# State space phase: a group's squares and state stores issued in the next group, its variances and normalization one chunk later

## The reference

```python
def step(h, inp):                       # one chunk
    decay = exp(where(causal, acum_l - acum_s, -inf))
    y = einsum((cc @ bc) * decay, xc) + einsum(cc, h) * exp(acum)
    h = exp(acum[-1]) * h + einsum(bc, to_end * xc)
    return h, y
y = y + d_skip * xs
y = y * silu(z)
y = y * rsqrt(mean(y * y over a group's 256 channels) + EPS)
y = y * norm_g                          # outputs: y, and the final h of prompt and samples
```

## Time and profile before

| | |
|---|---|
| median of three runs | 5301.94 us (5300.33 to 5302.54) |
| the profiled execution | 5307.53 us |
| its span, first to last instruction | 5305.7 us |
| busy share of the span | PE 87%, DVE 68%, ACT 34%, POOL 29% |
| mean granted TensorE clock | 0.93 |

### The profile page before, as it was taken

One profiled execution on the slowest core, in us unless ns is written; L12 is line 12 of the kernel. 1 busy time (PEld: TensorE's weight loads), 2 busy tenths in 40 slices (PEclk: granted clock), 3 DMA queues, 4 the chain that ended last, 5 costly groups with the idle time before them and its releaser, 6 DMA issues. The chain is left out here.

```text
span 5305.7 us, 83850 instructions
## 1 busy us (share of the span) xinstructions
PE 4605.5 (87%) x28787; PEld 4251.3 (80%) x28787; DVE 3586.0 (68%) x6877; ACT 1782.4 (34%) x3697; POOL 1526.5 (29%) x1356
## 2 busy tenths in 40 slices
PE   5999999788887969874888376999999999999995
PEld 3999999677775649873887366999999999999994
DVE  3011555454554641234599997999999999999997
ACT  3111333323232641111444394333333333333332
POOL 0000000111110000000000002777777777777773
PEclk8999999888887889997999798999999999999997
DMA  3332222222222232342999157999999999999995
GB/s 134 126 135 84 83 89 89 113 105 104 105 105 73 53 114 92 134 150 83 357 351 334 68 197 248 358 366 364 368 361 362 371 362 362 367 363 365 369 361 197
DMA packets 349645, 1170.31 MB, mean 221 GB/s; under 512 B 40000, under 2 KB 91328, under 8 KB 342080
## 3 DMA queue, kind: packets, MB, share of 16 engines
q0 software_dynamic: 147456, 536.94, 27.2%
q1 hardware_dynamic: 159328, 483.07, 25.6%
q10 hardware_dynamic: 42720, 148.52, 7.3%
HBM read 971.20 MB, written 197.46 MB: 220 GB/s over the span
## 5 line engine op out<-in xcount | busy, mean ns | idle before, releaser
L2027 POOL DMA_INDIRECT ex_vr<-in_expert_v,ex_at x512 | 655.2, 1280 | 229.8 <-issue 152.8
L2025 POOL DMA_INDIRECT ex_ur<-scr_u_rows,ex_at x512 | 594.2, 1161 | 312.0 <-DVE ex_ur L2202 131.5
L2210 DVE SCALAR_TENSOR_TENSOR ex_acc_rows<-ex_vr,ex_wt,ex_acc_rows 128x1024 f32<-128x1024 f32 x512 | 649.5, 1278 | 42.7 <-ACT ex_wt L2130 21.1
L2202 DVE SCALAR_TENSOR_TENSOR ex_ur<-ex_ur,h_rows 128x1024 f32<-128x1024 f32 x512 | 619.5, 1219 | 16.2 <-DMA ex_ur<-scr_u_rows,ex_at 15.8
L2019 POOL COPY ex_at<-picked_at 128x4 uint32 x128 | 71.1, 555 | 1633.4 <-POOLq L121 1633.0
L897 POOL TENSOR_TENSOR sd_cts<-sd_cT,sd_ea 128x512 f32<-128x512 f32 x72 | 92.3, 1282 | 1524.0 <-ACT sd_ea L855 1524.0
L2037 PE MATMUL ex_ps<-hd_hi,ex_u_hi 128*128 128x320 f32 x2048 | 471.0, 311 | 30.4 <-DVE ex_u_lo L2176 27.6
L2037 PE MATMUL ex_ps<-hd_lo,ex_u_hi 128*128 128x320 f32 x2048 | 467.9, 310 | 0.0
L2037 PE MATMUL ex_ps<-hd_hi,ex_u_lo 128*128 128x320 f32 x2048 | 467.9, 310 | 0.0
L2128 ACT ACTIVATE ex_gel<-ex_dot 128x1 f32<-128x1 f32 x512 | 103.9, 203 | 998.9 <-DVE ex_ur L2202 862.5
L447 DVE TENSOR_TENSOR pr_w_lo<-pr_w,pr_w_hi 128x1024 fp32r<-128x1024 f32 x58 | 71.1, 1225 | 508.6 <-ACT pr_w_hi L443 508.6
(11 more groups left out here) (381 smaller groups left out, 11394.5 us busy)
## 6 DMA issues: line engine op xcount, KB each, us to landing
pk_raw_u<-in_expert_u SPq DMA_DIRECT2D x128, 512.0 KB
scr_u_rows<-pk_rows_u ACTq DMA_DIRECT2D x128, 512.0 KB, 6.2
ex_u<-in_expert_u SPq DMA_DIRECT2D x128, 512.0 KB
ex_v<-in_expert_v SPq DMA_DIRECT2D x128, 512.0 KB
scr_gate<-gt_stage SPq DMA_DIRECT2D x10, 4096.0 KB
ex_gate<-scr_gate SPq DMA_DIRECT2D x32, 1280.0 KB
pr_w<-in_w_main SPq DMA_DIRECT2D x58, 512.0 KB, 4.5
scr_xbc<-pr_out ACTq DMA_DIRECT2D x32, 576.0 KB
```

The source lines that it names most:

```text
L2025: nc.gpsimd.indirect_dma_start(out=ur[:, s], out_offset=None, in_=scr["u_rows"], in_offset=by).then_inc(ur_in[s], 16)
L2027: nc.gpsimd.indirect_dma_start(out=vr[:, s], out_offset=None, in_=io["expert_v"].rearrange("j i d -> (j i) d"), in_offset=by).then_inc(vr_ ...
L2202: v.scalar_tensor_tensor(out=ur[:, s], in0=ur[:, s], scalar=1.0, in1=rows[:, s], op0=ALU.mult, op1=ALU.mult, accum_out=dot[:, m:m + 1]).th ...
L2210: v.scalar_tensor_tensor(out=acc_g[:, s], in0=vr[:, s], scalar=wt[:, m:m + 1], in1=acc_g[:, s], op0=ALU.mult, op1=ALU.add).then_inc(row_r[ ...
```

## The change

The squares leave the end of a group and stand behind chunk 0 of the next, the state stores behind its chunk 1. The sums of squares stand behind chunk 1 instead of 0, and root, reciprocal, spreading and scaling stand one chunk later each. The store of y, in chunk 7 before, stands at the end of the next group, behind its last gate piece. The order of everything else, and all semaphores and waits, are as before.

```diff
-        SPREAD = {3: (0, 2), 4: (2, NV)}
-        USED = {3: 0, 4: 1, 5: 2}
+        SPREAD = {4: (0, 2), 5: (2, NV)}
+        USED = {4: 0, 5: 1, 6: 2}
...
                     scan(i, s, c)
-                    if before and c == 0:
+                    if before and c == 1:
                         variances(*before)
...
                     if c == 2:
                         round_gate_weights(i, s, 1, before is None)
-                    if before and c == 2:
+                    if before and c == 0:
+                        squares(*before)
+                    if before and c == 1:
+                        store_states(*before)
+                    if before and c == 3:
                         roots(*before)
                     if c in TAKEN:
                         take_gates(i, s, TAKEN[c])
-                    if before and c == 7:
-                        store_y(*before)
                 for n in range(len(TAKEN), 2 * PIECES):
                     take_gates(i, s, n)
+                if before:
+                    store_y(*before)
+
+            def squares(i, s):
                 act.wait_ge(yg_r, i * 2 + s + 1 + START)
                 nc.scalar.activation(sq[:], y[:, s], ACT.Square).then_inc(sq_r, 1)
+
+            def store_states(i, s):
                 sample_states_done(act, i, s)
                 act.dma_start(... h0[:]).then_inc(hs_st, 16)
                 act.dma_start(... hp[:]).then_inc(hp_st, 16)
 
             over_groups(act, group)
+            squares(*FINAL)
+            store_states(*FINAL)
             roots(*FINAL)
             store_y(*FINAL)
...
-                    if last and c == 2:
+                    if last and c == 3:
                         reciprocals(*last)
```

## The result

The changed kernel takes 5367.24 us, the median of four runs (5362.13 to 5371.71). The kernel before took 5302.24 us in the same comparison. The ratio is 1.0118, with a 95% interval from 1.0103 to 1.0132: 65 us slower. The profiled execution spans 5362.0 us against 5305.7.

What follows compares the result with a forecast made beforehand. No engine is full; a chain between PE, DVE and ACT bounds each group. 8.6 + 47.6 + 0 + 9.2 - 2.2 + 0.5 = 63.7 us more gave 5366 us, range 5342 to 5393 for 8 in 10.

Steps and rivals of the forecast that it cites:

- The total: Whole kernel: 63.7 us slower, 5366 us; this forecast with its own bounds, 5350 to 5384, had chance 0.73.
- One announced sign: Whole groups: the distance between two groups' y times z should grow by 8 to 11 us.
- The running state's store makes the copy late: Chunk 0 on DVE: the copy waits for the store, 5.45 us later; 8.6 us for seven starts.
- The ledger's size for this term: Scan of chunk 1, delayed by the state store: 1.0 us in six starts, 2.6 in group 1.
- The sums behind chunk 1: PE between the scans of chunks 1 and 2, without a gap: 6.8 us per start, 47.6 for seven.
- The y store: Group's head: DVE waits for its landing, 2.3 us each at groups 2, 3, 5 and 7, 9.2 in all.
- it lies under ACT's gap in groups 4 and 6: Groups 4 and 6: the y store lands at 1294.8, covered by ACT's idle time where its loop goes back.
- Groups 4 and 6: Where ACT's loop goes back: the turn ends earlier, a gain of 1.1 us each, 2.2 for two.
- Squares, roots and scaling at no price: Squares behind chunk 0, and root, reciprocal, spreading, scaling one chunk later: price 0 in the forecast.
- The clock did not hold: Rival at chunk 2: the clock holds, sums cost 29 us instead of 47.6, 5347 us; chance 0.11.
- The y store was not slow: Rival at the group's head: the y store takes its median 9.6 us, 5395 us; chance 0.08.
- The rivals without a loss: Two rivals at the starts: within 0.2%, about 5305 us, or faster, 5273 us; chance 0.04 each.

Runs made afterwards that it cites:

- states_at_end: The changed kernel with the two state stores back at the end of a group, behind the y store: 5326.88 us, ratio 1.0040 to the kernel before.
- sums_early: The kernel before with the sums of squares ahead of the running sums of chunk 1, not behind the scan of chunk 0: 5280.50 us, ratio 0.9952.
- sums_alone: The kernel before with only sums of squares, root, reciprocal, spreading and scaling one chunk later: 5315.49 us, ratio 1.0017.
- stores_alone_later: The kernel before with state stores behind chunk 1 and four tiny copies ahead of ACT's first group: 5300.40 us, ratio 0.9989.
- branch_target_earlier: The kernel before with three small copies of group 0 done by VectorE instead of ScalarE: 5295.76 us, ratio 0.9981.

## Why the prediction was right, step by step

**The total** came out at 5367 against 5366. The runs bear out the mechanism, so it is not luck alone. That it agrees to 1 us is luck: the interval of the loss is 55 to 70 us wide, and several sizes were off and partly cancel. Over the seven starts, from the traces before and after:

| stretch | forecast | measured |
|---|---|---|
| y times z to the scan of chunk 1 (both stores, ACT's gap) | +15.6 us | +11.5 us |
| scan of chunk 1 to scan of chunk 2 (the sums) | +47.6 us | +50.9 us |
| scan of chunk 2 to the next y times z | 0 | -3.6 us |

One announced sign failed. The distance between two y times z was to grow by 8 to 11 us. It grew by 7.3, 7.6, 11.8, 4.6, 13.3, 3.4 and 10.6 us in groups 1 to 7, so only group 7 lies inside. Group 3 was also not typical of the starts: before, the scan of chunk 1 came 20.9 us after y times z there, and 18.5 to 20.0 in the four other ordinary ones.

**The running state's store makes the copy late.** Right: seven waits of 3.5 to 4.1 us. The copy was forecast 5.45 us late and is about 4.2 late in group 3, counted from DVE's first step, and 4.0 to 4.9 in the four other ordinary starts. The step that was mis-sized is the issue time: I put it 0.86 us after the start of the last exponential, and the trace shows it 0.75 us after the start of the first. The row's landing time held (the copy starts 3.77 us after the issue). In group 3 the scan of chunk 1 comes 16.26 us after DVE's first step, against 16.18, so plus 0.1 where 1.0 was forecast. In group 1 it is 15.19 against 13.82, plus 1.4 where 2.6 was forecast; L956 stands at 1031.15 there, and the scan here:

```profile
1046.34 0.70 PE L759 MATMUL sd_psY<-sd_cts,sd_h 128*64 128x128 f32 x4
```

The five ordinary starts together paid 5.3 us where 6.6 was forecast. The ledger's size for this term was therefore somewhat high.

**The sums behind chunk 1.** Right in kind, a little low in size: forecast 6.8 us per start, measured 7.3 on average. In group 3 it is 12.85 - 4.55 = 8.3: the 7.2 that the prediction worked out there, and 1.1 because the scan of chunk 1 itself now runs at the low clock, which the sum left out. Five starts paid 7.5 to 8.3 us, groups 2 and 7 only 5.3, where the clock stayed up through the sums.

**How the two belong together.** The sum had this right only as a total. It booked 8.6 us on the state's store and 47.6 on the sums. The runs show that neither is a price of its own: moved alone, the state stores cost nothing in the ordinary starts and the sums 9 us in all, and taking either one out of the changed kernel gives back 41 or 43 us. With the sums behind chunk 0, PE works while DVE waits. With the state's store early, the gates of chunk 1 move up by most of what the sums then cost. Only both together leave PE idle first and overloaded after.

**The y store.** Forecast 2.3 us in four groups with a landing of 4.2 us; the landing is 4.2 (median) and the delay 2.7 in group 3, 10.6 us in the four groups instead of 9.2. The step that failed is that it lies under ACT's gap in groups 4 and 6. The gap shrank, and there too DVE's wait is what ends last. Its removal gave 17 us, not 9.2.

**Groups 4 and 6.** A gain of 1.1 us each was forecast from an unchanged gap. Measured from y times z to the first copy L850, group 4 went from 11.75 to 9.61 us, 2.1 us gained. The gap itself fell to 2.6 us for a reason that the prediction did not have.

**Squares, roots and scaling at no price.** The squares are hidden in the changed kernel, as the ACT rows show. For the others there is no run of their own; behind the scan of chunk 2, where they stand, the seven groups lost nothing (the table).

**Rivals.** The clock did not hold (0.50 behind the sums in every start), though groups 2 and 7 came within 1.1 us of that rival's 4.2 us a start. The y store was not slow (4.2). The rivals without a loss needed a copy that does not wait or a PE that idles behind the scan of chunk 1. The price of the 128 KB store of the running state depends on what was issued ahead of it: its median is 3.7 to 4.2 us in twelve of the kernels, and 5.8 in states_at_end, where both the y and the 1 MB state go out just before.

## What to carry to other kernels

Before moving a store later, look for who overwrites its source, and on which engine that wait stands. Here a copy in the first chunk of the next group waited for it, and the gate weights behind the copy. Work that fills another engine's wait has no price until it is moved: cost the parts of a change together, and test them both by adding one alone and by taking one away. When work must be moved, move it into idle time that the timeline shows, as sums_early did for 0.5%.

## What the hardware showed that was not expected

ACT's loop going back cost 5.5 to 5.9 us or nearly nothing, by the place of its first instruction in ACT's program. Counted in ACT's compute instructions and transfers, each of the four exponentials by itself, the loop begins at row 272 in the kernel before, in sums_alone and in sums_early, and all three have the gap and 65 packets in the queue q14. It begins 1 to 3 rows earlier in the changed kernel and eight others, which show 55 or 56 packets and gaps of 0 to 4.8 us; most of such a gap is the issue of the transfers there, since states_at_end, with 4.0 and 4.8 us, has 3.4 in its ordinary starts as well. In stores_alone_later the loop begins at row 274, and the 65 packets are back. The Trainium skill (Runtime: NRT & Kernel Launch, Instruction fetch mechanics) says that a taken branch to code outside the fetched window forces a fetch before execution goes on. The packet counts agree with it: ten more in the queue of instructions where the gap is long. The gap was 1.8 to 2.1 us in stores_alone_later with no state store just issued, and 5.5 to 5.9 us behind a 1 MB store. That the gap is this fetch is read from the packets, and that the store's data delay it is argued from these two cases; no run shows either by itself.

The sums of squares, one column each, depend on the clock: 4.08 to 4.15 us for 36 instructions when the whole of them ran high, 7.68 us wholly at the low level. So a gap that is removed can come back in part as slower products behind it: of the 5.0 us by which the first copy of group 4 came earlier in branch_target_earlier, the distance to the next group kept 2.7.

A transfer can be issued ahead of compute instructions that stand before it in ACT's order. Here the first state store went out 0.3 us after the first of four exponentials had started (1229.29 to 1229.55).
